# A reordered tail of the expert stage, and a fifth row block of the up product in rounded parts

## The reference

```
hid = silu(einsum('td,edf->tef', t, w1)) * einsum('td,edf->tef', t, w3)
hid = hid * gate[..., None]
y = hid.reshape(T, N_EXPERTS * EXP_FF) @ w2.reshape(N_EXPERTS * EXP_FF, D_MODEL)
return y.reshape(bsz, s, dm)
```

## Time and profile before

| | |
|---|---|
| time of the profiled execution | 1217.04 us |
| its span | 1215.3 us |
| runs | 1217.58, 1217.92, 1219.41 us |
| mean granted TensorE clock | 0.988 |
| TensorE matmul busy | 1173.7 us |
| TensorE weight load busy | 869.2 us |
| VectorE busy | 719.7 us |
| ScalarE busy | 590.3 us |
| expert stage, layer 0 (first up product of item 1 to last add) | 425.4 to 604.1 us |
| expert stage, layer 1 (the same) | 1034.3 to 1212.2 us |

### The profile page before, as it was taken

How to read it: one execution, slowest core, us unless ns; L and a number is a source line. 1 busy time by engine, 2 the same in 40 slices (tenths; PEclk the granted TensorE clock), 3 DMA queues, 4 the chain that set the end, 5 groups by cost and what they waited for, 6 DMA issues and landing times.

```text
span 1215.3 us, 15456 instructions
## 1 busy us (share of the span) xinstructions
PE 1173.7 (97%) x5272; PEld 869.2 (72%) x5272; DVE 719.7 (59%) x1281; ACT 590.3 (49%) x1134; POOL 361.1 (30%) x320
## 2 busy tenths in 40 slices
PE   8999999999999899999899999989999998999996
PEld 5467876788777566666678887768887775666665
DVE  4797533322422688888745992772223236888887
ACT  2733246455634266655535364453456342666661
POOL 2034440564222011113136664263342220111130
PEclk9999999999999999999999999999999999999999
DMA  9432231277102799997232230012322018999963
GB/s 294 141 139 78 32 114 70 93 293 306 70 1 95 308 404 380 389 379 283 76 130 78 70 117 23 2 70 74 134 70 70 1 70 322 394 374 393 377 237 126
DMA packets 77643, 214.92 MB, mean 177 GB/s; under 512 B 23620, under 2 KB 24560, under 8 KB 65272
## 3 DMA queue, kind: packets, MB, share of 16 engines
q1 hardware_dynamic: 64688, 180.22, 40.0%
q0 software_dynamic: 10048, 28.92, 6.5%
q10 hardware_dynamic: 2840, 4.91, 1.1%
HBM read 187.90 MB, written 32.51 MB: 181 GB/s over the span
## 4 chain that ended last, share of the span: by engine, by line
PE 85%; DVE 7%; ACT 2%; DMA 2%; issue 2%; SPq 1%; DVEq 0%; ACTq 0%
PE bank L853 40%; PE bank L1212 7%; PE bank L1245 7%; PE bank L1217 6%; PE bank L1073 2%; PE bank L1095 2%; PE bank L891 2%; PE bank L826 2%; PE bank L1154 1%; PE bank L1201 1%; PE bank L1122 1%; PE bank L1034 1%; PE bank L1268 1%; SPq L611 1%; DVE h L2491 1%
## 5 line engine op out<-in xcount | busy, mean ns | idle before, releaser
L684 POOL TENSOR_TENSOR wlo<-W,whi 128x512 fp32r<-128x512 f32 x176 | 256.3, 1468 | 444.4 <-ACT whi L1477 426.3
L1477 ACT ACTIVATE whi<-W 128x512 fp32r<-128x512 f32 x176 | 108.1, 631 | 243.8 <-PE bank L853 225.6
L853 PE MATMUL bank<-whi,xTr 128*128 128x512 f32 x480 | 193.4, 403 | 0.9 <-ACT E L1941 0.7
L853 PE MATMUL bank<-wlo,xTr 128*128 128x512 f32 x416 | 162.9, 391 | 0.0
L853 PEld LDWEIGHTS bank<-whi,xTr 128*128 128x128 f32 x480 | 90.8, 189 | 21.8 <-POOL wlo L684 1.7
L853 PE MATMUL bank<-whi,E4r 128*128 128x512 f32 x256 | 99.8, 390 | 0.0
L1217 PE MATMUL bank<-E4r,E1r 128*128 128x512 f32 x360 | 98.5, 422 | 0.0
L1245 PE MATMUL bank<-whi,E2r 128*128 128x512 f32 x256 | 89.3, 410 | 7.4 <-DVE E2r L2452 5.9
L853 PEld LDWEIGHTS bank<-wlo,xTr 128*128 128x128 f32 x416 | 78.7, 189 | 16.6 <-issue 1.2
L2043 DVE TENSOR_TENSOR h<-bank,h 128x512 f32<-128x512 f32 x32 | 21.8, 692 | 115.0 <-PE bank L853 115.0
L1217 PEld LDWEIGHTS bank<-E4r,E1r 128*128 128x128 f32 x360 | 67.6, 188 | 27.0 <-issue 7.4
(11 more groups left out here) (498 smaller groups left out, 2422.7 us busy)
## 6 DMA issues: line engine op xcount, KB each, us to landing
E<-in_moe_w SPq DMA_DIRECT2D x48, 1024.0 KB, 11.5
W<-in_moe_w SPq DMA_DIRECT2D x32, 1024.0 KB, 9.7
xT<-in_moe_w SPq DMA_DIRECT2D x16, 1024.0 KB, 14.3
W<-in_od_w_in SPq DMA_DIRECT2D x7, 2048.0 KB, 8.4
ybuf<-E SPq DMA_DIRECT2D x26, 512.0 KB, 8.1
ybuf<-memV POOLq DMA_DIRECT2D x12, 1024.0 KB, 19.9
W<-in_w_mem_kv SPq DMA_DIRECT2D x4, 2048.0 KB, 9.3
W<-in_xa_wq SPq DMA_DIRECT2D x4, 2048.0 KB, 7.8
```

The lines of the kernel that those rows point to most:

```text
L684: pool.tensor_tensor(wlo[s_ % RING][:, :], slot(name)[:, block_of(name, k), :], whi[s_ % RING][:, :].bitcast(F32), ALU.subtract).then_inc( ...
L853: ins = pe.matmul(bank(u + t)[:, :], a, b, start=(k == 0 and n == 0), stop=(k == KT - 1 and n == 2))
L1477: act.activation(whi[s_ % RING][:, :], slot(name)[:, block_of(name, k), :], ACT.Copy).then_inc(S["w_hi"], 1)
```

## The change

`SPLIT` becomes 5: three full-precision blocks and five in rounded parts. The fifth high part lies in a free piece of E5, the fifth low part in `smr`, and the rows' parts are 640 columns wide. In the last quad, item 3's w2 parts go to the buffers of the up parts (`end_whi`, `end_wlo`), free by then, in place of `whi` and `wlo`. The order of the last items is changed on three engines.

```diff
-        xg_hi, xg_lo = v3(E1r, 4, 3072, 3584), v3(E1r, 4, 2560, 3072)
-        SPLIT = 4
-        up_hi = [E4r[:, 512 * c:512 * c + 512] for c in range(SPLIT)]
-        up_lo = [E4r[:, 2048 + 512 * c:2560 + 512 * c] for c in range(SPLIT)]
+        SPLIT = 5
+        xg_hi, xg_lo = v3(E1r, SPLIT, 3072, 3072 + SPLIT * P), v3(E1r, SPLIT, 3072 - SPLIT * P, 3072)
+        up_hi = [E4r[:, 512 * c:512 * c + 512] for c in range(4)] + [E5r[:, 4096:4608]]
+        up_lo = [E4r[:, 2048 + 512 * c:2560 + 512 * c] for c in range(4)] + [smr[:, 0:512]]
...
+        end_whi, end_wlo = up_hi[0:4], up_lo[0:4]
...
                     turn_hidden(q, 2, last=True)
-                    down(q, 2, late=1)
                     pe.wait_ge(S["late_onehots"], l + 1)
                     pe.wait_ge(m["xt_ready"], q * (2 * SLOTS) + 2 * SLOTS)
                     to_tokens(0, 0)
                     pe.wait_ge(m["hid_ready"], q * SLOTS + 3)
                     to_tokens(0, 1)
+                    down(q, 2, late=1)
                     turn_hidden(q, 3, last=True)
+                    down(q, 3, late=2)
                     to_tokens(1, 0)
                     to_tokens(1, 1)
-                    down(q, 3, late=2)
-                    for n in range(2):
-                        to_tokens(n, 2)
-                    for t in range(3):
-                        to_tokens(2, t)
+                    to_tokens(0, 2)
+                    to_tokens(1, 2)
+                    to_tokens(2, 0)
+                    to_tokens(2, 1)
+                    to_tokens(2, 2)
                     for n in range(3):
                         to_tokens(n, 3)
...
-                for n in range(LATE):
-                    item(last_quad, SLOTS - LATE + n, late=n)
+                item(last_quad, 1, late=True)
+                gated_hidden(last_quad, 2)
+                down_high(last_quad, 2, [w[:, :] for w in whi])
+                gated_hidden(last_quad, 3)
+                hidden_high(last_quad, 2)
+                down_high(last_quad, 3, end_whi)
+                late_high(last_quad, 2, 1)
+                hidden_high(last_quad, 3)
+                late_high(last_quad, 3, 2)
...
                     output(q, 0)
+                    late_tokens()
+                    late_onehot(0)
+                    late_onehot(1).then_inc(S["late_onehots"], 1)
                     hidden(q, 1)
                     low_parts(q, 1)
-                    late_onehots()
                     late_low(0, 0)
                     late_low(0, 1)
+                    hidden(q, 2)
+                    down_low(q, 2, *ring, last=True)
+                    late_onehot(2)
                     add_row(0, 0)
+                    hidden_low(q, 2, last=True)
+                    hidden(q, 3)
+                    down_low(q, 3, end_whi, end_wlo, last=True)
+                    late_low(1, 0)
+                    late_low(1, 1)
+                    hidden_low(q, 3, last=True)
                     add_row(0, 1)
-                    hidden(q, 2)
-                    low_parts(q, 2, last=True)
                     add_row(1, 0)
-                    late_low(1, 0)
                     add_row(1, 1)
-                    late_low(1, 1)
-                    hidden(q, 3)
-                    low_parts(q, 3, last=True)
+                    dve.wait_ge(m["y_stored1"], q * (8 * SLOTS))
+                    late_low(2, 0)
+                    late_low(2, 1)
+                    add_late(0)
                     add_row(2, 0)
+                    add_late(1)
                     add_row(2, 1)
                     add_row(3, 0)
-                    dve.wait_ge(m["y_stored1"], q * (8 * SLOTS))
-                    late_low(2, 0)
+                    add_late(2)
                     add_row(3, 1)
-                    late_low(2, 1)
-                    for t in range(TT):
-                        dve.wait_ge(S["late_filled"], TT * l + t + 1)
-                        for half, b in enumerate(token_banks[t]):
-                            hs = h[:, t, half * 512:(half + 1) * 512]
-                            ins = tt(hs, banks[b][:, :], hs, ALU.add)
-                        ins.then_inc(m["h_combined"], 1)
+                    add_late(3)
```

More of the change, by code:

```diff
@@ L1242, in down @@
                             xh, xl = hThi[par][:, k * P:(k + 1) * P], hTlo[par][:, k * P:(k + 1) * P]
-                            wh, wl = whi[2 * half + k], wlo[2 * half + k]
+                            wh, wl = (end_whi, end_wlo) if late == LATE - 1 else (whi, wlo)
+                            wh, wl = wh[2 * half + k], wl[2 * half + k]
                             for n, (a, b) in enumerate(((xh, wh), (xh, wl), (xl, wh))):
@@ L1777, in rows_high, with gated_hidden, down_high @@
                     act.activation(xg_hi, xgT[:, KT - SPLIT:KT, :], ACT.Copy).then_inc(m["hi_parts"], 1)
-                def item(q, j, late=None):
-                    par = j % 2
-                    last = late is not None and j > 1
+                def gated_hidden(q, j):
                     act.wait_ge(m["hid_filled"], q * SLOTS + (j + 1))
-                    act.activation(silu[par], banks[2 + par][:, 0:FF], ACT.Silu).then_inc(m["silu_ready"], 1)
+                    act.activation(silu[j % 2], banks[2 + j % 2][:, 0:FF], ACT.Silu).then_inc(m["silu_ready"], 1)
+                def down_high(q, j, dst):
                     act.wait_ge(m[f"w2_{j}"], q * 16 + 16)
@@ L1787, in item, with hidden_high @@
                         for k in range(2):
-                            act.activation(whi[2 * half + k][:, :], w2s[j][:, k, half * 512:(half + 1) * 512], ACT.Copy)\
+                            act.activation(dst[2 * half + k], w2s[j][:, k, half * 512:(half + 1) * 512], ACT.Copy)\
                                .then_inc(m["hi_parts"], 1)
-                    if not last:
-                        up_high(q, j + 2, 0, 2)
+                def hidden_high(q, j):
                     act.wait_ge(m["ht_filled"], q * SLOTS + (j + 1))
-                    act.activation(hThi[par], banks[4][:, 0:2 * P], ACT.Copy).then_inc(m["hi_parts"], 1)
@@ L1794, in item @@
[L1794 to L1804, removed]
+                    act.activation(hThi[j % 2], banks[4][:, 0:2 * P], ACT.Copy).then_inc(m["hi_parts"], 1)
@@ new lines, in late_high @@
+                def late_high(q, j, n):
+                    act.wait_ge(S["late_cols"], 2 * l + 1)
+                    if n == LATE - 1:
+                        act.wait_ge(m["y_stored0"], q * (8 * SLOTS) + 16)
+                    for half in range(2):
+                        act.wait_ge(m[f"y_filled{half}"], q * SLOTS + (j + 1))
+                        act.activation(late_hi[n][:, half * 512:(half + 1) * 512], banks[5 + half][:, :], ACT.Copy,
+                                       scale=late_gate[:, n:n + 1]).then_inc(S["late_hi"], 1)
@@ L1805, in item @@
+                def item(q, j, late=False):
+                    par = j % 2
+                    gated_hidden(q, j)
+                    down_high(q, j, [w[:, :] for w in whi])
+                    up_high(q, j + 2, 0, 2)
+                    hidden_high(q, j)
+                    up_high(q, j + 2, 2, SPLIT)
+                    rows_high(q, j + 2)
+                    if late:
+                        late_high(q, j, 0)
                         return
@@ L2439, in rows_low, with down_low @@
                     tt(xg_lo, xgT[:, KT - SPLIT:KT, :], xg_hi.bitcast(F32), ALU.subtract).then_inc(m["lo_parts"], 1)
-                def low_parts(q, j, last=False):
+                def down_low(q, j, high, low, last=False):
                     for half in range(2):
@@ L2491, in add_row, with add_late @@
                     v(stt(h[:, t, :], Yg[j][:, t, :], gate[:, j, t:t + 1], h[:, t, :], ALU.mult, ALU.add))
+                def add_late(t):
+                    dve.wait_ge(S["late_filled"], TT * l + t + 1)
+                    for half, b in enumerate(token_banks[t]):
+                        hs = h[:, t, half * 512:(half + 1) * 512]
+                        ins = tt(hs, banks[b][:, :], hs, ALU.add)
+                    ins.then_inc(m["h_combined"], 1)
                 def last_turn(q):
```

38 lines of the change are left out of this document (20 added, 18 removed).

## The result

The changed kernel takes 1211.1 us (median of 6 runs, 1208.93 to 1214.9) where the kernel before takes 1218.08 in the same rounds (6 runs, 1217.21 to 1223.47). The ratio is 0.9935, with a 95% interval from 0.9914 to 0.9957: 0.65% faster. Forecast were 1214.0 us and 0.32%. The direction is right and the time lies inside the range, but the gain is about twice the forecast.

A forecast was written before the change was run, and what follows sets the result against it. TensorE, busy nearly the whole span, was taken as the bound. 1217.0 - 4.1 + 2.2 - 1.7 - 2.8 = 1210.6 us; two clock drops give 1213.8, a few tenths for unseen waits 1214.0; range 1210.5 to 1218.6.

The forecast's parts named there:

- The fifth block in the items: Steady items of the expert stage: TensorE saves 0.17 us an item, 2.06 us a layer, -4.1 us in both.
- rival 4: Steady items: VectorE becomes the bound in each item, making the kernel slower, 1223.5 us; chance 0.06.
- The start, +1.1 twice: Start of each expert stage: TensorE pauses 1.7 us for VectorE's low parts, losing 1.1 us a layer, +2.2 us.
- the walk: The prediction's timetable of the changed kernel through the expert stage's start, items and end.
- The tail of layer 1, -1.7: After layer 1's last up product: the last add ends at +30.8 us, before at +32.5; -1.7 us.
- The tail of layer 0, -2.8: After layer 0's last up product: ScalarE's first read of the next norm at +31.2 us, before at +34.0; -2.8 us.
- The sum without any drop, 1210.6: Whole kernel: the profiled 1217.0 us plus the terms for items, starts and stage ends, without clock drops, gives 1210.6 us.
- Rival 3: End of the stage: the new order gives nothing, for instance because VectorE's chain is longer than walked; 1216.7 us; chance 0.1.
- The clock: Five new TensorE pauses in the expert stages and before the next norm cost 2.3 clock drops, 3.7 us.
- rival 2: The new TensorE pauses don't cost: none or one clock drop, 1210.6 to 1212.2 us; chance 0.17.

The follow-up runs named there:

- rows_first: The changed kernel with the two row adds of token tile 2 put ahead of VectorE's first add from the banks; 1206.29 us, ratio 0.9907.
- tail_only: The changed kernel with four rounded blocks again (SPLIT 4), so only the new order of the last items; 1211.99 us, ratio 0.9951.
- both: rows_first, with the first item of each stage done with four full-precision and four rounded blocks; 1204.2 us, ratio 0.9885.
- after: The changed kernel itself, as first measured and profiled; 1211.1 us, ratio 0.9935.
- before_busy: The kernel before with eight useless matmuls in TensorE's pause before the down product of item 2 in the last quad; 1216.05 us, ratio 0.9991.
- pause_plus1: The changed kernel with one repeat of the fifth block's subtraction on VectorE ahead of the rows' one at each stage start; 1210.1 us, ratio 0.9943.
- both_again: The same kernel as both, unchanged, in a later set of runs; 1206.19 us, ratio 0.9918.

## Why the prediction was right and wrong, step by step

- **The fifth block in the items**: held. The interval is 10.21 us, not 10.17. Down takes 2.89 and not 2.87, and 13 intervals give -1.8 a layer where -2.06 was forecast. The VectorE wait forecast at about 1.2 us is 1.32; rival 4 is out.
- **The start, +1.1 twice**: held, +1.11 and +1.10. The rounded matmuls start where the walk put them; the pause is 1.50, not 1.7, because the full-precision matmuls hold TensorE until 432.22. (The walk's own terms here add up to 434.5 and not 434.6, and the eight adds at the end of layer 1 from +20.7 on to +31.0 and not +30.8; neither slip matters.)
- **The tail of layer 1, -1.7**: held, -1.85. The pause before down 3 is 1.68 (1.9), VectorE's idle time 2.40 (2.5), the last add at +30.64 (+30.8).
- **The tail of layer 0, -2.8**: held up to the drop. Measured is -1.9, with a drop behind the 3.37 us pause. The drop costs 1.0 us there: ScalarE's read comes 1.44 us after the last add (604.82 to 606.26), and without a drop, in `rows_first`, 0.42 (599.90 to 600.32). Part of the slow transposes lies beside the last add. The six profiles of the new tail that have a drop there show 0.95 to 1.96 us from the last add to the read, the two without one 0.42: a drop costs 0.5 to 1.5 us here.
- **The sum without any drop, 1210.6**: the medians are 1211.1 and, in the second set, 1210.3. That they come so close is in part luck. The sum starts from the profiled 1217.04 us and not from the median of 1218.08, and the stages give 5.1 of the 7.0 us between the medians; no stage of these profiles accounts for the rest. Rival 3 is out.
- **The step that failed is "The clock"**: 0.4 of a drop for each of the four short pauses and 0.7 for the long one, 2.3 drops in all, 3.7 us, of which two drops, 3.2 us, went into the forecast. I took the rate of the old tail's pauses (1.77 and 2.21 us, two of four) for pauses of 1.5 to 1.7 us, as if their length didn't matter. None of the short ones dropped the clock in any profile. The long one did each time (3.36 to 3.41 us in five profiles), and its drop costs 1.0 us in this one, not 1.6. So the term measures 1.0 us. With it the sum is 1211.6, beside the 1211.9 of the milestones; the difference is the items' missing 0.5 us less 0.15 in layer 1's tail. This was rival 2, and its chance of 0.17 was too low.

The page of rival 2 (the Trainium skill, "TensorE: Matmul & The Clock Gate", section "Why this matters for your kernels") warns only of gaps clearly longer than the short ones. For 1.50, 1.68 and 2.35 us the traces agree; the drops behind 1.77 and 2.2 us in the old tail don't follow from it, and those led me away from it.

**What stays open.** Why pauses of one length drop in some executions and not in others (2.21 to 2.27 us in four of six, 2.35 in none of two, 2.78 in one of three). And how the 4 to 8 us of the tail alone divide. By the milestones of the table above, the stages of `tail_only`'s profile give only 2.2 of them (1.1 and 1.35 less in the tails, 0.2 more in starts and items), in part because it had a 6.8 us low stretch in layer 0; the other 3.6 us of the profiled difference lie in stretches whose code is the same and which had fewer drops in that execution. That the old tail has drops in most executions and a wait for gathered rows in some would make its mean cost larger than its one trace shows. This is argued, not shown.

## What to carry to other kernels

Walk the change with durations from the trace and keep the clock as a term of its own, sized by the length of each pause and by its place in this kernel's own records: in the expert stages the clock never dropped behind 1.5 to 1.7 us, sometimes behind 1.7 to 2.8, always behind 3 and more, and at another place, among other pauses, 1.46 us was enough in 6 of 24 cases. When a consumer engine waits at the end of a stage, first look at the order of the engine that feeds it: moving the parts that TensorE needs ahead of two adds that nobody waited for gave as much as rebuilding three engines' orders. And where an engine now idles before a wait, put independent work there, unless it meets another engine's work on the same memory.

## What the runs showed that I had not expected

- The runs of the kernel before in the three later sets spread over 1212.2 to 1223.4 us in 63 executions, and the spread follows the mean granted clock: 1223 at 0.983 and 0.984, a mean of 1218.1 at 0.990 (20 runs) and of 1215.3 at 0.993 (11 runs), 0.8 to 0.9 us for each 0.001.
- A low stretch of 3.4 us can begin where TensorE had no pause over 0.8 us just before, as at 1029 us in `both`. One of 13.6 us came in after's profile in the mixer, from 121.7 us on.
- Row adds of VectorE and subtractions of GpSimd slow each other, 1.28 to 2.2 or 2.3 us and 5.00 to 7.00. In the changed kernel one row add overlaps GpSimd's four subtractions, and GpSimd takes 6.03.
- In layer 0 the rows gathered for the last adds can come late: VectorE waited 2.78 us for them in `before_busy`, 2.14 in `pause_plus1` (whose tail then took 32.35 us), 1.15 in `both` and 1.82 in `both_again`, and not at all in after. So the changed kernel keeps the weak point: one such add still stands ahead of the low part of item 2's hidden rows, for which TensorE paused 1.35 us in `pause_plus1`.
